# First convolution tap of the second feed-forward on ScalarE, both additions from the banks ahead of the other taps

## What is computed

```python
def _conv_ffn(x, w_gate, w_up, conv_w, conv_b, w_down):
    a = x @ w_gate
    a = lax.conv_general_dilated(a, conv_w[:, None, :], window_strides=(1,), padding=[(CONV_WIDTH - 1, 0)],
                                 dimension_numbers=('NWC', 'WIO', 'NWC'), feature_group_count=a.shape[-1]) + conv_b
    return (jax.nn.gelu(a, approximate=True) * (x @ w_up)) @ w_down
```

## Time and profile before

| | |
|---|---|
| median of three runs | 915.97 us (913.98 to 916.34) |
| the profiled execution, its own time | 915.35 us |
| its span | 913.5 us |
| PE busy | 898.5 us (98%) |
| DVE busy | 673.4 us (74%), 1280 instructions |
| ACT busy | 467.5 us (51%), 938 instructions |
| POOL busy | 205.1 us (22%) |
| chain that ended last | PE 91%, DVE 5%, ACT 2% of the span |
| granted TensorE clock | 0.999 of full speed over the span |
| hidden steps of the second feed-forward | 32, from 649.4 to 900.4 us |

### The profile page before, as it was taken

One profiled execution on the slowest core, in us unless ns is written; L12 is line 12 of the kernel. 1 busy time (PEld: TensorE's weight loads), 2 busy tenths in 40 slices (PEclk: granted clock), 3 DMA queues, 4 the chain that ended last, 5 costly groups with the idle time before them and its releaser, 6 DMA issues.

```text
span 913.5 us, 16799 instructions
## 1 busy us (share of the span) xinstructions
PE 898.5 (98%) x6763; PEld 798.0 (87%) x6763; DVE 673.4 (74%) x1280; ACT 467.5 (51%) x938; POOL 205.1 (22%) x112
## 2 busy tenths in 40 slices
PE   9999999999999999999999999999999999999997
PEld 8979999889999888888888899887888888888886
DVE  6624997667556888777676768858888888788885
ACT  6434336574443574434444647776634355443443
POOL 4123421441212211652214432230110310210100
PEclk9999999999999999999999999999999999999999
DMA  8644443324343645655545454225355455455441
GB/s 296 223 139 164 161 147 129 117 97 149 129 139 124 228 180 184 230 184 212 193 157 222 138 203 163 94 87 204 103 183 225 162 177 219 180 216 191 166 166 47
DMA packets 23181, 153.67 MB, mean 168 GB/s; under 512 B 2864, under 2 KB 3248, under 8 KB 5568
## 3 DMA queue, kind: packets, MB, share of 16 engines
q1 hardware_dynamic: 22384, 150.43, 45.8%
q0 software_dynamic: 576, 2.10, 0.7%
q10 hardware_dynamic: 144, 0.07, 0.0%
HBM read 151.28 MB, written 1.05 MB: 167 GB/s over the span
## 4 chain that ended last, share of the span: by engine, by line
PE 91%; DVE 5%; ACT 2%; issue 1%; DMA 0%; DVEq 0%; SPq 0%; ACTq 0%
PE pb L519 89%; PE pb L522 2%; DVE wl L528 2%; ACT wh L525 1%; DVE FA L528 1%; ACT R L525 1%; DVE FA L531 0%; DMA X<-in_x 0%; DVE FA L534 0%; DVE FA L537 0%; DVE st L531 0%; DVE X L534 0%; ACT FA L525 0%; DVE R L534 0%; DVE wh L543 0%
## 5 line engine op out<-in xcount | busy, mean ns | idle before, releaser
L519 PE MATMUL pb<-R,wh 128*128 128x256 f32 (+2 forms) x2224 | 546.3, 325 | 3.8 <-DVE FA L528 1.6
L519 PE MATMUL pb<-R,wl 128*128 128x256 f32 (+1 forms) x1512 | 422.0, 281 | 0.0
L519 PEld LDWEIGHTS pb<-R,wh 128*128 128x128 f32 x2224 | 369.8, 189 | 42.9 <-ACT FA L525 3.3
L528 DVE TENSOR_TENSOR wl<-raw,wh 128x1024 fp32r<-128x1024 f32 (+1 forms) x206 | 272.1, 1344 | 85.4 <-ACT wh L525 83.8
L528 POOL TENSOR_TENSOR wl<-raw,wh 128x1024 fp32r<-128x1024 f32 (+1 forms) x72 | 176.5, 2456 | 601.1 <-ACT wh L525 449.9
L519 PEld LDWEIGHTS pb<-R,wl 128*128 128x128 f32 x1512 | 284.2, 188 | 1.7
L525 ACT ACTIVATE wh<-raw 128x1024 fp32r<-128x1024 f32 (+1 forms) x221 | 224.2, 1044 | 51.9 <-PE pb L519 49.2
L519 PE MATMUL pb<-wh,R 128*128 128x512 f32 (+2 forms) x724 | 234.5, 389 | 0.2 <-DVE wl L528 0.2
L519 PEld LDWEIGHTS pb<-wh,R 128*128 128x128 f32 (+1 forms) x724 | 134.4, 186 | 32.6 <-DVE wl L528 1.0
L525 ACT ACTIVATE FA<-pb 128x256 f32<-128x256 f32 (+7 forms) x240 | 94.0, 415 | 118.1 <-PE pb L519 107.0
L519 PE MATMUL pb<-wl,R 128*128 128x512 f32 (+2 forms) x372 | 143.3, 385 | 0.0
(11 more groups left out here) (122 smaller groups left out, 462.3 us busy)
## 6 DMA issues: line engine op xcount, KB each, us to landing
raw<-in_w SPq DMA_DIRECT2D x137, 1024.0 KB, 4.8
X<-in_x SPq DMA_DIRECT2D x2, 512.0 KB, 4.1
raw<-in_w SPq DMA_DIRECT2D x2, 512.0 KB, 6.8
post<-in_ffn_post SPq DMA_DIRECT2D x2, 512.0 KB, 3.9
post<-in_w POOLq DMA_DIRECT2D x2, 512.0 KB, 4.0
FA<-in_w POOLq DMA_DIRECT2D x2, 512.0 KB, 8.2
out<-X SPq DMA_DIRECT2D x4, 256.0 KB, 2.0
cst<-in_cst SPq DMA_DIRECT2D x1, 821.5 KB, 12.5
```

Source lines behind the costliest of these rows:

```text
L519: return self.real.matmul(*a, **k) if self.real else self
L528: return self.real.tensor_tensor(*a, **k) if self.real else self
```

## The change

ScalarE makes the first tap, as an activation Identity with a scale and a bias that are both read from `sm`; DVE no longer has the TENSOR_SCALAR. On DVE the two folds stand together, in front of the second and third tap, and the second tap waits for ScalarE's tap.

```diff
@@ scalar, step hidden
+                        e.wait_ge(*dve.at(("folded", *gate[1:])))
+                        e.activation(s0, fa(2048 + 256 * (i % 2), 256), ACT.Identity, bias=sc("conv_b", i),
+                                     scale=sc("conv_w", 64 + i)).then_inc(*act.up(("tap", i)))
                         e.wait_ge(*dve.at(("conv", i)))
                         e.activation(s0, s0, ACT.Gelu_apprx_tanh).then_inc(*act.up(("gated", name, i)))
@@ vector, step hidden
                         banks.ended(use, dve.now())
-                        if use == gate and name == "ffn2":
-                            cw = S_("conv_w").rearrange("p (i n) -> p i n", i=3)
-                            e.wait_ge(*dve.now())
-                            e.tensor_scalar(s0, g, cw[:, 2, i:i + 1], sc("conv_b", i), ALU.mult, ALU.add).then_inc(*dve.up())
-                            e.wait_ge(*dve.now())
-                            e.scalar_tensor_tensor(s0[:, 1:256], g[:, 0:255], cw[:, 1, i:i + 1], s0[:, 1:256], ALU.mult,
-                                                   ALU.add).then_inc(*dve.up())
-                            e.wait_ge(*dve.now())
-                            e.scalar_tensor_tensor(s0[:, 2:256], g[:, 0:254], cw[:, 0, i:i + 1], s0[:, 2:256], ALU.mult,
-                                                   ALU.add).then_inc(*dve.up(("conv", i)))
+                    if name == "ffn2":
+                        cw = S_("conv_w").rearrange("p (i n) -> p i n", i=3)
+                        e.wait_ge(*act.at(("tap", i)))
+                        e.scalar_tensor_tensor(s0[:, 1:256], g[:, 0:255], cw[:, 1, i:i + 1], s0[:, 1:256], ALU.mult,
+                                                   ALU.add).then_inc(*dve.up())
+                        e.wait_ge(*dve.now())
+                        e.scalar_tensor_tensor(s0[:, 2:256], g[:, 0:254], cw[:, 0, i:i + 1], s0[:, 2:256], ALU.mult,
+                                                   ALU.add).then_inc(*dve.up(("conv", i)))
                     e.wait_ge(*act.at(("gated", name, i)))
```

## The result

The changed kernel took 918.15 us, the median of 8 executions (916.59 to 918.61), beside 915.09 us for the kernel before (8 executions, 913.65 to 916.34). The ratio is 1.0034, with a 95% interval of 1.0025 to 1.0043: slower by 0.34%. The profiled execution took 917.8 us; its span is 916.0 us.

A forecast was written before the change was run, and what follows sets the result against it. The prediction took a closed loop of DVE and ACT to bound the kernel: 0.44 + 4.94 - 1.70 makes it 3.7 us late; less 0.60 of lead, PE ends 3.1 us later, median 919.0 us, range 915.8 to 920.6.

The forecast's parts named there:

- the case that I gave 0.62: Last feed-forward: DVE and ACT's loop falls behind, so PE ends 3.1 us later, median 919.0 us; chance 0.62.
- The loop of DVE and ACT: Making hidden tiles, DVE and ACT wait only for each other, so 0.1 us more per step takes 0.1 us of lead.
- The tap, T = 0.60 us: First tap on ACT: 0.42 us plus 91 ns each for scale and bias read from memory, 0.60 us.
- +0.19 us for an ordinary step, +0.44 for step 0: Gate fold to gelu: 2.13 us instead of 1.94 in 26 steps; 2.38 in hidden tile 0, with its table load.
- -0.34 us for a POOL step: Hidden tiles 2, 8, 11, 16, 20: POOL holds the second tap instead of the first; gelu 0.88 us behind POOL, not 1.22.
- Lead of 0.60 us, PE 3.1 us late: At hidden tile 31 the loop, 3.7 us late, has 0.60 us of lead over PE, so PE ends 3.1 us later.
- PE near the start, net +0.10: Near the feed-forward's start PE loses 0.63 us at 662.98 and wins 0.53 at 666.41, net +0.10.
- The moved fold: Fold of up put ahead of the taps: loop gains nothing; u2's bank free 1.4 us sooner, -0.53 us for PE at 666.41.
- PE waits at its last hidden tile and ends as much later, and what follows PE is unchanged: At the feed-forward's end PE waits for the late operand and ends 3.1 us later; what follows PE takes as long as before.
- PE hides it: Rival: tap costs less than two reads, or the loop has unseen lead; 915.7 to 916.6 us, no change; chance 0.26.
- The second tap isn't held: Rival: POOL doesn't hold the second tap, 1.43 us gained five times, 7.2 us; 916.1 us, not slower; chance 0.05.
- New holds: Rival: in the later loop DVE's wl or casts meet POOL's work elsewhere, up to 2 us each; 920.5 to 922; chance 0.07.

The follow-up runs named there:

- The five steps alone: Change made only in hidden tiles 2, 8, 11, 16, 20, where POOL works, other steps as in the kernel before: 914.76 us, ratio 0.9993.
- my own reordering: Against the kernel with the change only in hidden tiles 2, 8, 11, 16, 20: DVE's last cast ahead of each of tiles 2 to 9 moved behind it; 913.54 us, ratio 0.9996.

## Why the prediction was right, point by point

919.0 us was forecast and 918.15 measured; slower by 0.34% lies in the case that I gave 0.62, though I had held a slower kernel (0.48) no likelier than one that can't be told from the kernel before (0.48).

- **The loop of DVE and ACT is closed and bounds.** Right. The tap without its two operands, 0.18 us less on ACT for each tile, takes the whole loss away, although PE is 98% busy in all of these kernels.
- **The tap, T = 0.60 us.** Right: 602 ns in the mean of 32, so two operands cost what two single ones do. The group of the page of the changed kernel (busy, mean ns, idle before):

```profile
L525 ACT ACTIVATE FA<-FA,sm 128x256 f32<-128x256 f32 x32 | 19.3, 602 | 66.9 <-DVE FA L528 66.9
```

- **+0.19 us for an ordinary step, +0.44 for step 0.** Right: 0.19 and 0.42. 26 times 0.19 is what makes the case. In step 0 the table load took 1.28 us and the gelu started 0.01 us behind its end, as the row of before had it.
- **-0.34 us for a POOL step.** The mechanism is right, the hold moved from the first tap to the second; the second tap took 1.52 us and not about 2, as it started later, which changes nothing in the sum. The size was 0.39, since the gelu starts 0.84 us behind POOL and not 0.88: the second tap ended 0.29 behind it, where I had scaled 0.27 to 0.33 (0.27 x 0.49 / 0.43 is 0.31). This and step 0 make the sum 3.4 instead of 3.7; measured were 3.30. The five steps alone, run by themselves, gave 0.39 each and nothing else. The rule of the Trainium skill (SBUF — State Buffer, "Who interferes with whom") that a DVE instruction with two SBUF inputs contends with a GpSimd instruction that reads SBUF is borne out by that tap, which takes 0.48 us alone and took 1.52 beside POOL.
- **Lead of 0.60 us, PE 3.1 us late.** Right in kind: 3.30 - 0.60 = 2.70, and PE was 2.70 us late. The stop itself is 1.87 us, a little under the 2 to 3 of the forecast, since PE was already 0.64 us late.
- **PE near the start, net +0.10.** Right there (+0.04), and incomplete. I had asked only where PE stops, not where it nearly stops. At 720.63 us PE was held again, by the gate fold of hidden tile 9 (720.12 to 720.53), and fell from 0.04 to 0.64 us behind; before, that fold ended at 721.67 and PE went on at 722.03, some 0.2 us later than it could have. It changed nothing in the sum, since the later stop contains it, but in a kernel whose tail had more lead it would have been the whole result.
- **The moved fold: nothing for the loop, 0.53 us for PE.** Right for the loop. For PE the gain is 0.2 us and not 0.53 (it is 0.24 us late without the move, 0.04 with it), because without it the longer first stop already covers most of the second.
- **PE waits at its last hidden tile and ends as much later, and what follows PE is unchanged.** What follows PE's last matmul is unchanged, 5.9 us in both profiles. The step that failed is the one before: PE's work behind the stop was taken to be as fast as ever, without a term for the clock. In two of three profiles the clock fell behind the stop, 1.57 us more, so that an execution loses some 2.7 or 4.3 us; 3.06 us between the medians lies between the two. That the forecast of 3.1 us came so near is in part luck: the missing term and the 0.4 us that the sum had too much pull in opposite directions, and the medians carry the start besides.
- **919.0 against 918.15 us.** This 0.85 us is the base: I added 3.1 us to a median of three executions (915.97), and eight executions of the same kernel gave 915.09.
- **The rivals.** *PE hides it* fell with T = 0.60. *The second tap isn't held* fell with its 1.52 us. *New holds* did not come in the change; they did in my own reordering, where a cast took 2.2 us longer beside POOL, so that the mechanism is real.

## What to carry to other kernels

Where two engines hand work to each other and wait for nobody else, an instruction belongs on the engine that does it in less time including its hand-over, whatever their busy shares say: here 16 us less on DVE made PE 2.7 us late. Before moving work, list the margins of the bounding engine at each place where it could wait, not only its stops, and compare the change summed over the steps with the margin at the last one. An instruction that depends on nothing belongs where its engine waits for another anyway: the cast taken out of such a wait exposed 0.53 us. And before two profiles are compared, align them at an event just ahead of the changed stage: the spans here differ by 2.5 us where the loss is 4.39.

## What was not expected of the hardware

- **The clock after a stop.** Stops of 1.87 us of PE in the tail were followed by a granted clock of 0.50 in two of three profiles of the same program, and cost 1.57 us more; stops of 1.69 us at 661.66 and of 1.85 and 1.86 us at 663.56 and 903.79 (tap on ACT, fold of up not moved) were not followed by one.
- **An independent DVE instruction between two dependent ones cost half of its time.** A fold of 0.42 us delayed what followed by 0.21 us (656.18 to 656.84, against 649.35 to 649.80), since two independent ones overlap: 0.75 us for the pair.
- **A DVE instruction with one input is held by POOL too.** The TENSOR_SCALAR of before (2.02 us) and a cast (2.89 us for 0.69) both ended just behind POOL's `wl` (0.14 and 0.55 us).
- **The start of the work differs by 2 us and more**, at the first projection already (10.12 to 13.07 us over 14 profiles), which is more than most differences looked for here. The same 24 matmuls ahead of it took 2.94 to 5.49 us; where the trace has the granted clock of that stretch, it is 0.50.
